# Input rows laid out turned by the host, a second weight chunk in quarters, and memory row factors kept for the third block

## The chip, the core and the metric

The kernel runs on one core of a Trainium2 chip. The metric is the device time of one execution in microseconds (us). The engines that matter here are TensorE (PE in the profile; PEld is its weight load), VectorE (DVE), ScalarE (ACT), GpSimd (POOL), and SyncE (SP), which issues all loads. Loads are moved by 16 DMA engines. Tiles live in SBUF, results of PE in eight PSUM banks.

## The reference

The program is a small two-layer model over one sequence of 256 rows with 1024 features, and 256 rows of memory that every layer attends to:

```python
def rms_norm(x, gain):
    xf = x.astype(jnp.float32)
    y = xf * lax.rsqrt(jnp.mean(xf * xf, axis=-1, keepdims=True) + RMS_EPS)
    return (y * gain.astype(jnp.float32)).astype(x.dtype)

def memory_cross_attention(h, m, w_q, w_kv, w_o, q_norm, k_norm):
    k, v = _split(m @ w_kv, (MEM_HEADS * MEM_HEAD_DIM, MEM_HEADS * MEM_HEAD_DIM))
    ...

def first_block(x, mem, ...):
    for i in range(DEPTH):                      # DEPTH = 2
        h = rms_norm(x, norm_mix[i])
        if i % 2 == 0:
            x = x + dsa_moba_mixer(h, ...)       # block 1: its first product is h @ ab_w_in, 1024 x 2472
        else:
            x = x + nsa_mixer(h, ...)            # block 3
        x = x + memory_cross_attention(rms_norm(x, norm_mem[i]), rms_norm(mem, norm_mem_src[i]), ...)
        x = x + swiglu(rms_norm(x, norm_ffn[i]), ffn_w_in[i], ffn_w_out[i])    # with memory: blocks 2 and 4
    return x

def reference(x, mem, positions, ...):
    x = first_block(x, mem, positions, ...)
    return second_block(x, ...)                  # blocks 5 to 8: two layers of branches and a feed-forward
```

x and mem enter a product only after rms_norm, and the mean square of a memory row is the same in both layers, since mem never changes. The kernel makes the memory's keys and values of layer 0 in block 1, those of layer 1 in block 3.

## The kernel before

**Products.** Every product is computed in three matmuls of split numbers: a weight w is rounded to w_hi by ACT (L143) and the remainder w_lo = w - w_hi is formed by DVE (L144); the features are split in the same way into h_hi and h_lo. PE then adds h_hi w_hi, h_hi w_lo and h_lo w_hi (L456 to L458 in `Project`, L890 to L892 in `MemoryRows`). Here a group is a feature tile of 128 features and a tile of 128 rows; the 256 rows are two tiles.

**Weights.** `Weights` cuts the weight matrices into chunks of 1 MB (four feature tiles by 512 columns). SP loads the chunks in program order into four raw slots; ACT (`round_to`) and DVE (`cut_to`) fill three slots of halves ahead of PE. A chunk is 24 matmuls of 512 columns. Chunk c goes to ACT when it has landed and the chunk that used its slot is consumed. `FirstChunk` (L208 to L249) handles chunk 0 apart: two loads of half a chunk, and four quarters of 512 columns that ACT rounds (L232) and DVE cuts (L240) one by one, so that PE can begin on the first.

**Features.** `Features` makes h_hi and h_lo of 256 rows. PE turns the rows by 16 transposes into PSUM (`turn`, L279), ACT scales by the gain and rounds (L297), DVE takes the remainder (L303). The row factor of rms_norm is not multiplied in there: ACT squares the rows and sums (L290), three small POOL operations (L312 to L318) make the factor, and it is applied when a product is copied out of its bank (L470 on ACT, L484 on DVE).

**Block 1**, `block_dsa_moba`, is where the program starts. SP loads x, the gains, chunk 0 in halves, chunks 1 to 3, a gain, the positions, the memory rows, then the other chunks as slots come free (`load_all`). `Project` takes two chunks for each block of 512 output columns: chunks 0 and 1 give the first block, 2 and 3 the second. PE does 16 dummy transposes (L1400), turns x, and does the chunks; what it does between chunks is written by hand: after chunk 1 the memory rows are turned, after chunk 3 the index heads are turned (L393, `turn_index`), and the index scores (L1410) follow later. On ACT the order is: features and chunk 0's quarters, chunk 1, the squares of x, chunk 2, the sines of the rope tables (L1036, L1037), the first copy out (L470), chunk 3, the memory rows (L297) and their squares, chunk 4. On DVE: features and quarters, chunk 1, the rope tables (L1051 to L1069, a chain of small steps), chunk 2, the copy out (L484), chunk 3, the memory rows (L303), chunk 4. On POOL the factors of x come first, then the memsets of the rope frequencies (L1031), for which DVE's rope tables wait. All queues run in order: what stands behind a waiting instruction waits with it.

**Block 3**, `block_nsa`, has memory rows of its own again: SP loads them (L870), ACT squares them, POOL makes the factors, PE turns them (L279) ahead of small matmuls (L2323), ACT and DVE split them (L297, L303), and `MemoryRows.pe` (L890) uses them. POOL's head norm (L674), DVE's use of it (L656) and small matmuls of compressed tokens (L2268) stand near that work.

## Time and profile before

| | |
|---|---|
| median of 3 runs | 1661.8 us (1661.35 to 1661.95) |
| span of the profiled execution | 1659.6 us |
| PE busy | 1619.1 us, 98% |
| DVE busy | 1096.3 us, 66% |
| ACT busy | 891.3 us, 54% |
| POOL busy | 421.5 us, 25% |
| read from memory | 262.52 MB |

The span is the time in which the profiler saw the core's instructions; the device time of a run holds a little more, 2.2 us at the median. Times in rows count from the start of the span. A row of the timeline gives the start, the busy time, the engine, the line, the operation, its output and inputs, and how many instructions it sums up; what stands in brackets is how long the engine was idle just before, and what ended that.

### The profile page before, as it was taken

Reading aid. Unit: us, or ns where it says so; the run is one execution under the profiler, and the core shown is the slowest. Engines: PE = TensorE matmul, PEld = TensorE weight load, DVE = VectorE, ACT = ScalarE, POOL = GpSimd, SP = SyncE. Lnnn points to the kernel's source line nnn. Section 1 sums busy time; section 2 is a strip of 40 time slices with the busy share of each in tenths; the row PEclk is TensorE's granted clock in tenths of the full one; section 3 lists DMA queues with packets and bytes.
Section 4 is the critical chain, followed back from the end, with each engine's and each line's share of the span. In section 5 each row is a group of like instructions: output and inputs, shape, how many; then the busy total and the mean of one; then the engine's idle time right before and its main releaser. Section 6 shows DMA issues by size and latency. Waiting matters only on the chain. (4 is left out here: it accounts for less than half of the span.)

```text
span 1659.6 us, 26949 instructions
## 1 busy us (share of the span) xinstructions
PE 1619.1 (98%) x10929; PEld 1462.8 (88%) x10929; DVE 1096.3 (66%) x1546; ACT 891.3 (54%) x1401; POOL 421.5 (25%) x460
## 2 busy tenths in 40 slices
PE   8999999999999999999999999999999999999999
PEld 7767899987887889998889998999888999999997
DVE  6875665645576665655577768777646876867763
ACT  6465554434455555443456746566445684756652
POOL 2500100002341120000147802244204690214430
PEclk9999999999999999999999999999999999999999
DMA  7523376556330236665555444766556444376652
GB/s 278 174 77 101 103 205 194 185 197 213 99 135 27 77 102 172 185 186 193 174 195 164 147 133 147 189 185 190 181 154 220 159 153 130 131 204 187 190 179 76
DMA packets 287067, 265.30 MB, mean 160 GB/s; under 512 B 12256, under 2 KB 247520, under 8 KB 286944
## 3 DMA queue, kind: packets, MB, share of 16 engines
q1 hardware_dynamic: 286944, 263.59, 50.8%
q8 instruction: 86, 1.41, 0.4%
q14 instruction: 37, 0.30, 0.1%
HBM read 262.52 MB, written 1.05 MB: 159 GB/s over the span
## 5 line engine op out<-in xcount | busy, mean ns | idle before, releaser
L144 DVE TENSOR_TENSOR w_lo<-w_raw,w_hi 128x2048 fp32r<-128x2048 f32 (+2 forms) x244 | 565.8, 2321 | 288.6 <-ACT w_hi L143 283.6
L143 ACT ACTIVATE w_hi<-w_raw 128x2048 fp32r<-128x2048 f32 (+2 forms) x244 | 462.9, 1902 | 214.6 <-PE bank L529 125.5
L1873 PE MATMUL bank<-h_hi,w_hi 128*128 128x256 f32 x1984 | 565.5, 285 | 4.7 <-issue 1.2
L1874 PE MATMUL bank<-h_lo,w_hi 128*128 128x256 f32 x1984 | 561.3, 283 | 0.0
L1875 PE MATMUL bank<-h_hi,w_lo 128*128 128x256 f32 x1984 | 561.2, 283 | 0.0
L1873 PEld LDWEIGHTS bank<-h_hi,w_hi 128*128 128x128 f32 x1984 | 380.5, 192 | 8.2 <-issue 7.5
L1874 PEld LDWEIGHTS bank<-h_lo,w_hi 128*128 128x128 f32 x1984 | 380.7, 192 | 0.1
L1875 PEld LDWEIGHTS bank<-h_hi,w_lo 128*128 128x128 f32 x1984 | 380.6, 192 | 0.0
L456 PE MATMUL bank<-w_hi,h_hi 128*128 128x512 f32 (+1 forms) x288 | 113.4, 394 | 5.4 <-DVE w_lo L144 3.3
L2953 POOL TENSOR_TENSOR cffn_hidden<-cffn_conv 128x256 f32<-128x256 f32 x44 | 73.7, 1675 | 155.5 <-ACT cffn_conv L2984 155.5
L457 PE MATMUL bank<-w_lo,h_hi 128*128 128x512 f32 (+1 forms) x288 | 111.9, 388 | 0.0
L458 PE MATMUL bank<-w_hi,h_lo 128*128 128x512 f32 (+1 forms) x288 | 111.7, 388 | 0.0
L2531 POOL TENSOR_TENSOR mix_conv<-mix_conv,mix_gates 128x512 f32<-128x512 f32 x60 | 105.2, 1752 | 24.4 <-ACT mix_gates L2568 17.2
L1770 ACT ACTIVATE mf_gate<-mf_gate 128x256 f32<-128x256 f32 x44 | 18.4, 418 | 129.8 <-DVE mf_gate L1819 129.8
L3018 DVE SCALAR_TENSOR_TENSOR cffn_conv<-cffn_before,cffn_cols,cffn_conv 128x255 f32<-128x255 f32 x176 | 75.0, 488 | 0.0
L456 PEld LDWEIGHTS bank<-w_hi,h_hi 128*128 128x128 f32 x288 | 54.2, 188 | 18.8 <-DVE w_lo L144 4.2
L458 PEld LDWEIGHTS bank<-w_hi,h_lo 128*128 128x128 f32 x288 | 54.2, 188 | 10.9
L457 PEld LDWEIGHTS bank<-w_lo,h_hi 128*128 128x128 f32 x288 | 54.2, 188 | 10.1
L3006 DVE TENSOR_TENSOR cffn_before<-bank,cffn_row_factors 128x512 f32<-128x512 f32 x44 | 30.4, 691 | 49.4 <-PE bank L1875 48.7
L2482 POOL MEMSET mix_padded<- 128x572 f32 x2 | 1.2, 577 | 240.4 <-POOLq L1728 187.2
L778 ACT ACTIVATE mix_att<-mix_att,mix_att_stat 128x256 f32<-128x256 f32 x48 | 24.0, 502 | 61.5 <-PE bank L750 40.0
L526 PE MATMUL bank<-w_lo,cffn_wide_hi 128*128 128x512 f32 x144 | 56.0, 389 | 0.0
(447 smaller groups left out, 2858.0 us busy)
## 6 DMA issues: line engine op xcount, KB each, us to landing
w_raw<-in_w_in SPq DMA_DIRECT2D x48, 1024.0 KB, 5.0
w_raw<-in_ffn_w_in SPq DMA_DIRECT2D x88, 512.0 KB, 5.0
w_raw<-in_w_up SPq DMA_DIRECT2D x88, 512.0 KB, 5.2
w_raw<-in_ffn_w_out SPq DMA_DIRECT2D x22, 1024.0 KB, 4.9
w_raw<-in_w_down SPq DMA_DIRECT2D x22, 1024.0 KB, 5.0
w_raw<-in_nsa_w_in SPq DMA_DIRECT2D x10, 1024.0 KB, 5.2
w_raw<-in_mem_w_kv SPq DMA_DIRECT2D x8, 1024.0 KB, 5.1
w_raw<-in_w_branch SPq DMA_DIRECT2D x8, 1024.0 KB, 5.1
```

Source lines behind the costliest of these rows:

```text
L143: return act.activation(hi, raw, ACT.Copy)
L144: return dve.tensor_tensor(self.lo[:, cut_slot, 0:k * n], raw, hi.bitcast(F32), ALU.subtract)
L456: pe.matmul(bank, x_hi, whi[:, k, :], start=(f == 0), stop=False)
L457: pe.matmul(bank, x_hi, wlo[:, k, :], start=False, stop=False)
L458: ins = pe.matmul(bank, x_lo, whi[:, k, :], start=False, stop=(f == KD - 1))
L526: pe.matmul(self.bank[2 * t + half][:, :], x_hi, wlo[:, k, columns], start=False, stop=False)
L1873: pe.matmul(out, h, hi[:, f, :], start=(f == 0), stop=False)
L1874: pe.matmul(out, h, lo[:, f, :], start=False, stop=False)
L1875: ins = pe.matmul(out, l, hi[:, f, :], start=False, stop=(f == KD - 1))
L2531: pool.tensor_tensor(conv[:, :, :], conv[:, :, :], taps[tap % 4], ALU.add).then_inc(cv_sum, 1)
L2953: pool.tensor_tensor(hidden[:, j % 2, :], conv[:, j % 2, 0, :], conv[:, j % 2, 1, :], ALU.mult)\
L3018: dve.scalar_tensor_tensor(out=dst, in0=src, scalar=tap(2 * side, tile), in1=dst, op0=ALU.mult, op1=ALU.add).then_inc(sides, 1)
```

## The change

The host also passes x and mem laid out turned, as 128 features by 8 tiles by 256 rows (`x_turned`, `mem_turned`). `Features` with `laid` reads such a tile in SBUF instead of the banks, and PE turns neither x nor the memory rows, in block 1 or in block 3. The rows themselves are still loaded in block 1, for the squares and for the residual sum; x's rows now come after chunk 2 in SP's queue, behind both halves of x_turned, chunk 0 and chunk 1. The dummy transposes become 20. `FirstChunk` is made for chunks 0 and 1, so chunk 1 too is loaded in halves and split in quarters; FIRST_ORDER says which features are rounded and cut ahead of which quarter. Chunk 2 is rounded ahead of the squares of x on ACT, behind which there is now a wait for x's rows, and cut ahead of the rope tables on DVE. The memory rows' factors are kept in `mem_stat` beside the memory's keys and values, so block 3 has no squares, no factor steps and no load of the rows (it loads `mem_turned` instead, as many bytes).

```diff
@@ FirstChunk
-    def __init__(self, k, chunk):
-        s, self.w, (self.rows, self.n, sources) = k.sems, k.weights, chunk
+    def __init__(self, k, chunk, c):
+        s, self.w, self.c, (self.rows, self.n, sources) = k.sems, k.weights, c, chunk
...
@@ Features
     def view(self, f):
+        if self.laid is not None:
+            return self.laid[:, f, :]
         return self.k.bank[(self.bank + f // 2) % 8][:, (f % 2) * S:(f % 2) * S + S]
...
         for f in features:
-            if not self.first:
+            if self.laid is not None:
+                if self.landed:
+                    act.wait_ge(self.landed[f // 4], 16)
+            elif not self.first:
                 act.wait_ge(self.turned, self.turns[f // 4])
...
@@ MemoryRows
-    def turn(self, pe):
-        pe.wait_ge(self.rows_in, 16)
-        self.features.turn_all(pe)
-
     def load(self, sp):
-        sp.dma_start(self.rows, self.source.rearrange("(t p) d -> p t d", p=P)).then_inc(self.rows_in, 16)
+        sp.dma_start(self.turned, self.a["mem_turned"]).then_inc(self.turned_in, 16)
+        if self.layer == 0:
+            sp.dma_start(self.rows, self.a["mem"].rearrange("(t p) d -> p t d", p=P)).then_inc(self.rows_in, 16)
...
-                self.features.wait_feature(pe, 1 if f == 0 and self.sums[0] == self.bank else f)
+                self.features.wait_feature(pe, f)
...
@@ block_dsa_moba
+        FIRST_ORDER = [(0, 1, 2), (3,), (4, 5), (6,), (7,), (), (), ()]
...
             def _(sp):
-                sp.dma_start(k.x[:, :, :], a["x"].rearrange("(t p) d -> p t d", p=P)).then_inc(x_in, 16)
                 sp.dma_start(k.gains_1[:, :], a["cols_1"]).then_inc(cols_in, 16)
                 for part in range(2):
-                    first.load(sp, part)
-                for c in range(1, w.EARLY):
-                    w.load(sp, w.chunks[c], w.raw_slot(c), w.early_in[c])
+                    features = slice(4 * part, 4 * part + 4)
+                    sp.dma_start(x_turned[:, features, :], a["x_turned"][:, features, :]).then_inc(x_landed[part], 16)
+                    first[0].load(sp, part)
+                for part in range(2):
+                    first[1].load(sp, part)
+                w.load(sp, w.chunks[2], w.raw_slot(2), w.early_in[2])
+                sp.dma_start(k.x[:, :, :], a["x"].rearrange("(t p) d -> p t d", p=P)).then_inc(x_in, 16)
+                w.load(sp, w.chunks[3], w.raw_slot(3), w.early_in[3])
...
@@ ACT
-                for i in range(3):
-                    rows.round(act, range(2 * i, 2 * i + 2))
-                    first.round(act, i)
-                first.round(act, 3)
-                rows.round(act, range(6, KD))
-                w.round_to(act, 1)
+                for i, features in enumerate(FIRST_ORDER):
+                    rows.round(act, features)
+                    first[i // 4].round(act, i % 4)
+                w.round_to(act, 2)
+                act.wait_ge(x_in, 16)
                 for t in range(T):
                     for part in range(2):
                         rows.square(act, t, part)
-                w.round_to(act, 2)
                 rope_tables.act(act)
...
@@ DVE
+                for i, features in enumerate(FIRST_ORDER):
+                    rows.cut(dve, features)
+                    first[i // 4].split(dve, i % 4)
+                w.cut_to(dve, 2)
                 rope_tables.dve(dve)
...
@@ PE
-                for i in range(16):
+                for i in range(20):
                     pe.transpose(k.bank[i // 4][:, i % 4 * P:i % 4 * P + P], k.ident[:, :], k.ident[:, :])
-                pe.wait_ge(x_in, 16)
-                rows.turn_all(pe)
...
                 def index(pe, j, part):
-                    if (j, part) == (0, 1):
-                        mem.turn(pe)
                     if (j, part) == (1, 1):
-                        pe.wait_ge(mem.features.lo_done, KD)
                         turn_index.pe(pe, lambda pe, i: hn.wait_done(pe, 2) if i < 2 else pe.wait_ge(doubled, 1))
...
@@ block_nsa
-        mem = MemoryRows(k, a, 1, feat[:, 0:8, :].rearrange("p (t a) b -> p t (a b)", t=T),
-                         [double[:, t, :, :].rearrange("p a b -> p (a b)") for t in range(T)], h_hi, h_lo, bank=0,
-                         sums=(0, 1, 3, 3))
+        mem = MemoryRows(k, a, 1, feat[:, 0:8, :], None, None, h_hi, h_lo, sums=(0, 1, 3, 3))
...
-                mem.features.factors(pool, 2)
...
-                        mem.act_square(act)
...
-                mem.turn(pe)
```

What stands in a row on the queues at the start of block 1, by the kernel's lines, shows the moves. SP, before (in_x is x, in_ab_w_in the weights of chunks 0 and on, ab_feat the tile that takes the memory rows):

```order
L1204 DMA x_rows<-in_x 128x2x1024
L1205 DMA gains<-in_cols 128x68
L221 DMA w_raw<-in_ab_w_in 128x2x512 x2
L126 DMA w_raw<-in_ab_w_in 128x4x512 x3
L1210 DMA ab_gain<-in_rows 128x256
L1026 DMA ab_pos_i<-in_positions 128x2
L870 DMA ab_feat<-in_mem 128x2x1024
```

SP, now:

```order
L1213 DMA gains<-in_cols 128x68
L1216 DMA ab_feat<-in_x_turned 128x1024
L221 DMA w_raw<-in_ab_w_in 128x2x512
L1216 DMA ab_feat<-in_x_turned 128x1024
L221 DMA w_raw<-in_ab_w_in 128x2x512 x3
L126 DMA w_raw<-in_ab_w_in 128x4x512
L1221 DMA x_rows<-in_x 128x2x1024
L126 DMA w_raw<-in_ab_w_in 128x4x512
L1223 DMA ab_gain<-in_rows 128x256
L1033 DMA ab_pos_i<-in_positions 128x2
L874 DMA ab_mem_turned<-in_mem_turned 128x2048
L876 DMA ab_feat<-in_mem 128x2x1024
```

x's rows moved from the front to a place between chunks 2 and 3, and two loads of 1 MB are new. ACT from the end of chunk 0's quarters to the round of chunk 4, before (ab_att takes the squares that nobody reads, ab_mem_hi the rounded memory features):

```order
L143 ACTIVATE w_hi<-w_raw 128x2048
L290 ACTIVATE ab_att,row_stat<-x_rows 128x512 x4
L143 ACTIVATE w_hi<-w_raw 128x2048
L1036 ACT_TABLE_LOAD
L1036 ACTIVATE rope_tables<-ab_cos_in 128x32
L1037 ACTIVATE rope_tables<-ab_sin_in 128x32
L470 ACTIVATE ab_proj<-bank,row_stat 128x512
L143 ACTIVATE w_hi<-w_raw 128x2048
L641 ACTIVATE ab_squares<-ab_proj 128x128
L297 ACTIVATE ab_mem_hi<-bank,gains 128x256 x8
L290 ACTIVATE ab_att,ab_mem_stat<-ab_feat 128x1024 x2
L143 ACTIVATE w_hi<-w_raw 128x2048
```

The same stretch of ACT now, from chunk 1's quarters on:

```order
L232 ACTIVATE w_hi<-w_raw 128x512 x4
L143 ACTIVATE w_hi<-w_raw 128x2048
L293 ACTIVATE ab_att,row_stat<-x_rows 128x512 x4
L1043 ACT_TABLE_LOAD
L1043 ACTIVATE rope_tables<-ab_cos_in 128x32
L1044 ACTIVATE rope_tables<-ab_sin_in 128x32
L477 ACTIVATE ab_proj<-bank,row_stat 128x512
L143 ACTIVATE w_hi<-w_raw 128x2048
L648 ACTIVATE ab_squares<-ab_proj 128x128
L303 ACTIVATE ab_mem_hi<-ab_mem_turned,gains 128x256 x8
L293 ACTIVATE ab_att,mem_stat<-ab_feat 128x1024 x2
L143 ACTIVATE w_hi<-w_raw 128x2048
```

The round of chunk 2 moved ahead of the squares of x; that of chunk 3 stands where it stood, behind the sines and the first copy out. DVE from chunk 1 to chunk 3, before (the small steps of the rope tables between):

```order
L144 TENSOR_TENSOR w_lo<-w_raw,w_hi 128x2048
L1051 CAST ab_pos<-ab_pos_i 128x2
L1052 CAST ab_pos<-ab_row_i 128x2
L1054 TENSOR_SCALAR ab_ang<-ab_inv,ab_pos 128x8 x4
L1057 TENSOR_SCALAR ab_turns<-ab_ang 128x32
...
L1069 TENSOR_SCALAR ab_cos_in<-ab_cos_in 128x32
L144 TENSOR_TENSOR w_lo<-w_raw,w_hi 128x2048
L484 TENSOR_SCALAR ab_proj<-bank,row_stat 128x512
L144 TENSOR_TENSOR w_lo<-w_raw,w_hi 128x2048
```

DVE now, from chunk 1's quarters:

```order
L240 TENSOR_TENSOR w_lo<-w_raw,w_hi 128x512 x4
L144 TENSOR_TENSOR w_lo<-w_raw,w_hi 128x2048
L1058 CAST ab_pos<-ab_pos_i 128x2
L1059 CAST ab_pos<-ab_row_i 128x2
L1061 TENSOR_SCALAR ab_ang<-ab_inv,ab_pos 128x8 x4
L1064 TENSOR_SCALAR ab_turns<-ab_ang 128x32
...
L1076 TENSOR_SCALAR ab_cos_in<-ab_cos_in 128x32
L491 TENSOR_SCALAR ab_proj<-bank,row_stat 128x512
L144 TENSOR_TENSOR w_lo<-w_raw,w_hi 128x2048
```

Chunk 2's cut moved from behind the rope tables to ahead of them; chunk 3's stays behind.

## Rows read from the trace of the kernel before

**Rows 1.** The page's head: span, and busy time, share, instructions by engine.

```profile
span 1659.6 us, 26949 instructions
PE 1619.1 (98%) x10929; PEld 1462.8 (88%) x10929; DVE 1096.3 (66%) x1546; ACT 891.3 (54%) x1401; POOL 421.5 (25%) x460
```

**Rows 2.** Timeline of PE, first 45 us: start, busy, instruction, idle before.

```profile
5.81 2.73 PE L279 MATMUL bank<-ident,x_rows 128*128 128x128 f32 x16
10.27 0.47 PE L456 MATMUL bank<-w_hi,h_hi 128*128 128x512 f32 x1 [1.72 <-DVE w_lo L240]
...
17.07 0.50 PE L456 MATMUL bank<-w_hi,h_hi 128*128 128x512 f32 x1 [1.02 <-DVE w_lo L144]
...
22.68 1.91 PE L279 MATMUL bank<-ident,ab_feat 128*128 128x128 f32 x16
...
31.05 0.39 PE L456 MATMUL bank<-w_hi,h_hi 128*128 128x512 f32 x1
...
37.07 0.48 PE L456 MATMUL bank<-w_hi,h_hi 128*128 128x512 f32 x1
...
43.65 0.72 PE L1410 MATMUL bank<-ab_feat 32*128 32x128 f32 x8 [0.89 <-DVE ab_feat L422]
```

**Rows 3.** Loads of chunks 1 to 3 (issue, landing), then windows: PEclk, share, GB/s.

```profile
L126 SPq DMA_DIRECT2D w_raw<-in_ab_w_in x3: 489/574/1427, 2.8 to 3.9; - x3
...
DMA to landing us min/median/max: 8.5/10.7/12.8
...
10.00:15.00 5.00, 4.74 (x21) 3.74 (x22) 4.56 (x11) 5.00 (x9) 0.00 (x0) 1.00 1.05 387
```

**Rows 4.** Timeline of ACT, first 35 us.

```profile
8.50 0.63 ACT L232 ACTIVATE w_hi<-w_raw 128x512 fp32r<-128x512 f32 x1
...
14.54 0.67 ACT L290 ACTIVATE ab_att<-x_rows 128x512 f32<-128x512 f32 x1
...
23.13 0.23 ACT L1036 ACTIVATE rope_tables<-ab_cos_in 128x32 f32<-128x32 f32 x1 [2.90 <-DVE ab_cos_in L1069]
...
23.95 1.90 ACT L143 ACTIVATE w_hi<-w_raw 128x2048 fp32r<-128x2048 f32 x1
...
31.33 1.97 ACT L143 ACTIVATE w_hi<-w_raw 128x2048 fp32r<-128x2048 f32 x1
```

**Rows 5.** Timeline of POOL and DVE, first 45 us.

```profile
17.20 0.20 POOL L312 TENSOR_TENSOR row_stat<-row_stat 128x2 f32<-128x2 f32 x1 [15.18 <-ACT ab_att L290]
...
18.92 0.49 DVE L1051 CAST ab_pos<-ab_pos_i 128x2 f32<-128x2 int32 x1 [1.91 <-POOL ab_inv L1031]
...
26.00 2.29 DVE L144 TENSOR_TENSOR w_lo<-w_raw,w_hi 128x2048 fp32r<-128x2048 f32 x1
...
43.09 0.42 DVE L422 COPY ab_feat<-bank 128x256 f32<-128x256 f32 x1
```

**Rows 6.** Block 3: windows (PEclk, third from the end), and PE's timeline.

```profile
424.00:427.00 3.00, 3.00 (x21) 2.74 (x20) 1.10 (x1) 0.00 (x0) 1.85 (x2) 0.50 0.24 49
...
472.00:475.00 3.00, 3.00 (x8) 2.34 (x7) 2.96 (x8) 0.85 (x1) 2.71 (x9) 0.50 0.00 0
...
422.10 4.29 PE L2268 MATMUL bank<-nsa_att,nsa_cmp_w 128*64 128x75 f32 x32 [1.42 <-issue]
...
472.07 0.63 PE L891 MATMUL bank<-w_lo,h_hi 128*128 128x512 f32 x1
...
472.50 0.63 PE L892 MATMUL bank<-w_hi,h_lo 128*128 128x512 f32 x1
```

**Rows 7.** Timeline of block 3 near the memory rows, PE and DVE.

```profile
419.49 2.51 DVE L2194 COPY nsa_att<-bank 64x510 f32<-64x510 f32 x4
...
465.59 1.97 PE L279 MATMUL bank<-ident,nsa_feat 128*128 128x128 f32 x16
...
468.84 0.94 DVE L656 TENSOR_TENSOR nsa_proj<-nsa_proj,nsa_hn_stat 128x512 f32<-128x512 f32 x1 [1.53 <-POOL nsa_hn_stat L674]
...
471.57 0.70 PE L890 MATMUL bank<-w_hi,h_hi 128*128 128x512 f32 x1 [0.52 <-DVE h_lo L303]
```

More of the change, by code:

```diff
@@ L251, with __init__ @@
 class Features:
-    def __init__(self, k, name, src, gain, hi, lo, scratch, bank, first=0, stat=None, parts=2):
+    def __init__(self, k, name, src, gain, hi, lo, scratch, bank=0, first=0, stat=None, parts=2, laid=None, landed=()):
         s = k.sems
+        self.laid, self.landed = laid, landed
         self.k, self.src, self.gain, self.hi, self.lo, self.scratch = k, src, gain, hi, lo, scratch
@@ L301, in cut @@
         for f in features:
-            dve.wait_ge(self.hi_done, f - f % 2 + 2 - self.first)
+            dve.wait_ge(self.hi_done, f + 1 if self.laid is not None else f - f % 2 + 2 - self.first)
             dve.scalar_tensor_tensor(out=self.lo[:, f, :], in0=self.view(f), scalar=self.gain[:, f:f + 1],
@@ L442, in pe @@
             for c in range(self.first[j], self.last[j] + 1):
-                if c or self.tiles is None:
+                tiles = self.tiles[c] if self.tiles is not None and c < len(self.tiles) else None
+                if tiles is None:
                     w.wait_cut(pe, c)
@@ L450, in pe @@
                         self.features.wait_feature(pe, f)
-                    if c == 0 and self.tiles is not None:
-                        self.tiles.wait_cut(pe, k)
+                    if tiles is not None:
+                        tiles.wait_cut(pe, k)
                     for t in range(T):
@@ L843, with __init__ @@
 class MemoryRows:
-    def __init__(self, k, a, layer, rows, scratch, hi, lo, bank=4, sums=(3,)):
+    def __init__(self, k, a, layer, turned, rows, scratch, hi, lo, sums=(3,)):
         s = k.sems
-        self.k, self.rows, self.hi, self.lo, self.source = k, rows, hi, lo, a["mem"]
-        stat = k.small("mem_stat", [P, 5, T])
-        self.rows_in, self.summed, self.copied = s("mem_in"), s("mem_summed"), s("mem_copied")
+        self.k, self.layer, self.turned, self.rows, self.hi, self.lo, self.a = k, layer, turned, rows, hi, lo, a
+        self.rows_in, self.turned_in = s("mem_in"), s("mem_turned_in")
+        self.summed, self.copied = s("mem_summed"), s("mem_copied")
         gain = k.gains_1[:, (2 + 4 * layer) * KD:(3 + 4 * layer) * KD]
-        self.features = Features(k, "mem_rows", rows, gain, hi, lo, scratch, bank, stat=stat, parts=1)
-        self.bank, self.sums = bank, sums
+        self.features = Features(k, "mem_rows", rows, gain, hi, lo, scratch, stat=k.mem_stat, parts=1, laid=turned,
+                                 landed=[self.turned_in] * 2)
+        self.sums = sums
     def add_chunks(self, w):
@@ L1121, in block_dsa_moba @@
         gains_in, const = s("gains_in"), s("const")
-        rows = Features(k, "rows", k.x, k.gains_1[:, 0:KD], h_hi, h_lo, k.norm_scratch, 4)
+        x_in, cols_in, filled = s("x_in"), s("cols_in"), s("filled")
+        x_turned, x_landed = feat[:, 8:16, :], [s("x_turned_in0"), s("x_turned_in1")]
+        rows = Features(k, "rows", k.x, k.gains_1[:, 0:KD], h_hi, h_lo, k.norm_scratch, laid=x_turned, landed=x_landed)
         after = Features(k, "after", k.x, k.gains_1[:, KD:2 * KD], h_hi, h_lo, k.norm_scratch, 4)
@@ L1308, in _ @@
             def _(dve):
-                for i in range(3):
-                    rows.cut(dve, range(2 * i, 2 * i + 2))
-                    first.split(dve, i)
-                first.split(dve, 3)
-                rows.cut(dve, range(6, KD))
-                w.cut_to(dve, 1)
+                for i, features in enumerate(FIRST_ORDER):
+                    rows.cut(dve, features)
+                    first[i // 4].split(dve, i % 4)
+                w.cut_to(dve, 2)
                 rope_tables.dve(dve)
```

29 lines of the change are left out of this document (16 added, 13 removed).

## The prediction

> **What bounds the kernel now.** I read the page's head first. The program is one core's chain of matrix work: PE is busy 98% of a span of 1659.6 us [rows 1]. A change can win only what PE waits for or no longer does, and only as far as nothing later takes it back. So I read the places that the diff touches: the first 45 us of block 1, and block 3 around its memory work.
>
> In the first 45 us, PE's timeline gives the stages and its waits [rows 2]. x lands at 5.8, PE turns it until 8.54 and waits 1.72 us for the first features and weights; the products start at 10.27. A chunk is 24 matmuls; chunk 1 runs from 17.07 to 22.68, 5.6 us or 0.23 us a matmul. Chunk 1 waited 1.02 us for DVE's w_lo, then come 1.91 us of memory turns, and chunk 3 starts at 31.05 with no wait beside its row. Chunk 4 starts at 37.07. The index scores at 43.65 wait 0.89 us for DVE's copy at 43.09 [rows 2, 5]; that copy hangs on the end of chunk 3 through the projection's copies.
>
> Loads come next. Issue time plus time to landing of the three whole chunks (2.8 + 8.5, 3.9 + 12.8) gives 11.3 and 16.7 for chunks 1 and 3, so 2.7 us for each MB, in the order of issue; the DMA engines are full (1.05) in 10 to 15 us [rows 3]. A load placed earlier delays by 2.7 us per MB all that is placed behind it.
>
> Last ACT, POOL and DVE, since the rows of x matter there for their mean square. ACT squares x at 14.54, POOL's factors start at 17.20 on the last square, the memsets of the rope frequencies stand behind them, DVE's rope tables start at 18.92 on those memsets, ACT's sines at 23.13 wait for DVE, and ACT rounds chunk 3 at 23.95 only after the sines and a copy [rows 4, 5]. DVE cuts it from 26.00 to 28.29 [rows 5], 2.76 us before PE wants it at 31.05. That slack is what the change spends.
>
> **The change part by part.** The span is 2.2 us shorter than the median of 1661.8 us; I work in the span's times and apply the difference to the median.
>
> *x loaded turned.* PE loses 16 turns, 2.73 us [rows 2], and the wait that followed. In total 1 MB lies ahead of the first half of chunk 0 (half of x_turned, half of the chunk), which is what lay ahead of 5.8 us before. ACT's first rounding of weights, at 8.50 before [rows 4], can then start near 5.9, and from it to the first matmul the old trace takes 10.27 - 8.50 = 1.8 us: first matmul near 7.7, **2.5 us earlier**. The four more dummy transposes cost nothing: at the 2.73 / 16 = 0.17 us of a turn they are 0.7 us, and PE is free from 5.6. With no such cover they would cost those 0.7. ACT and DVE read these features from SBUF now; the nearest rows are the same instructions from PSUM, and a few tenths either way lie under the matmuls of a feature (6 x 0.23 = 1.4 us).
>
> *Chunk 1 in quarters.* Its second half lands at 11.3 as before; the last four quarters need ACT's 0.63 us [rows 4] and something like that on DVE each, so the last is cut near 13.3, and the first well before chunk 0 ends (7.7 + 5.6 = 13.3). The wait of 1.02 goes: chunk 1 starts near 13.4, **3.7 us earlier**, and ends near 19.0.
>
> *Chunk 2 and the turns of the memory rows.* Chunk 2 still lands at 14.0 (11.3 + 2.7); 1.9 us of rounding (the row of chunk 3's) and 2.29 of cutting end at 18.3, under chunk 1. The 1.91 us of turns are gone. Chunk 2 follows chunk 1 at 19.0 and ends near **24.5**.
>
> *Where that gain goes.* x's rows were first in the queue; now gains, x_turned and chunks 0 to 2 are ahead, 4 MB, so they land where chunk 3 landed, at 16.7 [rows 3]. ACT's explicit wait for them stands ahead of the squares, which begin some 0.2 us after the landing (as PE did at 5.81, rows 2), near 16.95 instead of 14.54: 2.4 us later. Behind that wait on ACT are the sines, the copy and chunk 3's rounding; on POOL the factors and the memsets; on DVE, behind its wait for the memsets, the tables and chunk 3's cut. Each keeps its old distance:
> - squares to POOL's factors 17.20 - 14.54 = 2.66: 19.6;
> - POOL to the tables 18.92 - 17.20 = 1.72: 21.3;
> - tables to sines 23.13 - 18.92 = 4.21: 25.5;
> - sines to chunk 3's rounding 0.82, rounding 1.90: 28.3;
> - cut 2.29: **30.6**, and PE can start chunk 3 near 30.7.
>
> Before, it started at 31.05. Of the 6.5 us that PE gained, 0.35 is left; PE stands idle some 6.2 us, from 24.5 to 30.7, for DVE's cut of chunk 3.
>
> *Chunk 4.* It lands later, since turned memory rows and one more MB (x) stand ahead, but its rounding on ACT comes after that of chunk 3, the memory rounds and two squares. From the end of chunk 3's rounding (23.95 + 1.90 = 25.85) to the start of chunk 4's (31.33) are 5.5 us [rows 4]; so at the latest 28.3 + 5.5 = 33.8, rounded 35.7, cut 38.0. Before, PE came to chunk 4 at 37.07, 6.0 us after chunk 3's start, so now it comes at 36.7 and waits up to 1.3 us for chunk 4. That wait is covered by the 0.89 us at the index scores and the 0.35 by which their chain, which goes by the end of chunk 3, comes earlier. Net without the clock: **-0.3**, from 1661.8 to 1661.5.
>
> *The clock.* The 1.72 us of waiting from 8.54 on left the granted clock at 1.00 in 10 to 15 us [rows 2, 3]. But in block 3, 1.42 us of waiting and 32 small matmuls stand ahead of a granted clock of 0.50 in 424 to 427, and 0.52 us of waiting, at 471.57, ahead of 0.50 in 472 to 475 [rows 6, 7]. That is 1.2 GHz. A wait of 6.2 us is much longer than any here, so I take it that chunk 3 starts at half speed. The price is read from the second fall: 8 matmuls in 3.00 us, 0.43 us from one start to the next (472.07, 472.50) instead of 0.23, so 8 x 0.2 = **1.6 us** lost. From below the cost is 0 (the clock isn't lowered, or is back at once), from above all 24 matmuls of chunk 3, 24 x 0.2 = 4.8. I take 1.6, the one row that shows this kind of matmul after a fall. Chunk 3's end goes by it, so the index chain too: -0.3 + 1.6 = **+1.3**.
>
> The Trainium skill, page TensorE: Matmul & The Clock Gate, section HAM oscillation — how this bites in real kernels, says the same against this change: waits on PE between bursts send it back to half speed, and each next burst begins slow. Without that rule and with the first 45 us alone as witness the sum would be 1661.5; with it, 1663.1. No row of this trace has a wait of such length.
>
> *Block 3.* PE loses 16 turns (1.97 us at 465.59), ACT two squares and POOL three small operations. Nothing behind them is waiting for them. The small matmuls that follow on PE may start 1.9 us earlier, but the memory products at 471.57 wait for DVE's h_lo, and DVE stands behind its row at 468.84, which waited 1.53 us for POOL's head norm [rows 7]. That chain doesn't use the memory rows. Earlier, the matmuls at 422.10 wait 1.42 us for DVE's copies (419.49 + 2.51 = 422.00), not for ACT's squares [rows 6, 7]. So 1.9 us more of waiting, and 0 in the sum. Bounds: the whole 1.9 gained, if h_lo isn't what is late; or a longer stretch at half speed, since PE waits 2.4 us there instead of 0.5: at most a second price of 1.6 lost. The loads are as many bytes as before.
>
> **Sum**: -0.3 + 1.6 + 0 = +1.3 us, 1661.8 to **1663.1 us**: PE does 6.6 us less and stands that much longer.
>
> **The rivals.**
> - *No clock cost.* The clock comes back at once, or isn't lowered: 1661.5. For it: no fall after 1.72 us at the start. Against: two falls in block 3 after less.
> - *Slower: the low clock holds for all of chunk 3.* Then 24 matmuls lose 4.8 us, and the index chain comes 4.8 - 0.35 = 4.45 us later: **1666.2**. It is slower by over 3.3 us from (3.3 + 0.35) / 0.2 = 18 matmuls on. For it: chunk 3 is the first work after a full stop. Against: the fall at 472 was over after 8.
> - *Faster: x's rows don't hold chunk 3.* If x lands by some 13 us although it is issued behind 4 MB, its chain ends before 28.3 as it did before, and chunk 3 goes on at 25 or 26; then chunk 4 holds PE. That lands four loads of 1 MB behind 16.7 (chunk 3, the memory rows twice, itself), at 27.5, with the small loads between some 28.6; with 1.9 and 2.29 PE starts it at 33 instead of 37.07: -4.1, **1657.7**. For it: everything but x's rows is early enough. Against: the landings go by order of issue [rows 3], and the program waits for x explicitly.
> - *Block 3 pays.* 1.9 us come off there: 1663.1 - 1.9 = 1661.2. Against: the row at 471.57 names h_lo.
>
> The Trainium skill, page DMA: Bandwidth & Descriptors, section Queues, rings and completion order, says that completion is not first in, first out per issuing engine. By that x could land ahead of chunk 2, and the time would go towards the third rival's. Rows 3 here show the landings in order and 2.7 us apart.
>
> **How the numbers follow.** Forecast 1663.1: 0.52; no clock cost: 0.18; block 3 pays: 0.10; slower by the clock: 0.14; faster by an early x: 0.06. A measurement of this kernel can tell about 0.2%, 3.3 us. The first three are all within that: same 0.80, slower 0.14, faster 0.06. The range leaves out the last two cases and takes in the block 3 case without a clock cost (1659.6, nearly) and a second price in block 3 or a somewhat longer low stretch: **1660.0 to 1665.3**.
>
> **What would show it right or wrong.** In the changed trace: PE's first matmul near 7.7, chunk 1 near 13.4, chunk 2 near 19; ACT's squares near 17, DVE's tables near 21, chunk 3's cut near 28.3 to 30.6; on PE a wait of 6 us ahead of chunk 3 with DVE w_lo as its end, a granted clock of about 0.5 right behind it; index scores near 45; in block 3 a wait of over 2 us ahead of the memory products. It is wrong if x's squares start before 15, if chunk 3 starts before 29 or after 32, or if its matmuls start 0.23 us apart from the first.

## The result: 1668.4 us, slower by 0.4%

The changed kernel takes 1668.39 us at the median of 5 runs (1667.06 to 1668.69), the kernel before 1661.79; the ratio is 1.0039, with a 95% interval of 1.0027 to 1.0051. The forecast was 1663.1 us, with a range up to 1665.3. The profiled execution has a span of 1667.0 us, 7.4 more than before; it is the highest of the five runs, so the stages below add up to 7.4 and not to the 6.6 between the medians.

The page's head of the changed kernel, as [rows 1]:

```profile
span 1667.0 us, 26864 instructions
PE 1620.5 (97%) x10885; PEld 1460.6 (88%) x10885; DVE 1097.8 (66%) x1549; ACT 891.1 (53%) x1400; POOL 420.7 (25%) x457
```

TensorE has 44 instructions less and is busy 1.4 us longer. Its timeline in the first 47 us, as [rows 2]:

```profile
8.06 0.47 PE L463 MATMUL bank<-w_hi,h_hi 128*128 128x512 f32 x1 [1.65 <-DVE w_lo L240]
...
13.90 0.39 PE L463 MATMUL bank<-w_hi,h_hi 128*128 128x512 f32 x1
...
19.34 0.43 PE L463 MATMUL bank<-w_hi,h_hi 128*128 128x512 f32 x1
...
31.33 0.79 PE L463 MATMUL bank<-w_hi,h_hi 128*128 128x512 f32 x1 [6.33 <-DVE w_lo L144]
31.92 0.63 PE L464 MATMUL bank<-w_lo,h_hi 128*128 128x512 f32 x1
32.35 0.63 PE L465 MATMUL bank<-w_hi,h_lo 128*128 128x512 f32 x1
...
46.49 0.72 PE L1417 MATMUL bank<-ab_feat 32*128 32x128 f32 x8 [0.85 <-DVE ab_feat L428]
```

Chunk 2 starts 6.1 us earlier than before (19.34 against 25.48), and chunk 3 0.28 later, behind a wait of 6.33 us. Its matmuls start 0.43 us apart. The granted clock there (third from the end of a row of the windows):

```profile
25.00:30.00 5.00, 0.00 (x0) 0.00 (x0) 2.80 (x7) 3.88 (x8) 2.56 (x7) 0.97 1.05 399
30.00:33.00 3.00, 1.67 (x4) 1.38 (x5) 3.00 (x7) 3.00 (x7) 2.92 (x6) 0.50 1.03 356
33.00:36.00 3.00, 3.00 (x8) 2.32 (x8) 1.78 (x5) 3.00 (x5) 1.73 (x4) 0.50 0.95 358
36.00:40.00 4.00, 4.00 (x21) 3.29 (x21) 2.76 (x2) 0.58 (x2) 0.00 (x0) 0.93 0.17 29
```

So 12 of chunk 3's 24 matmuls ran at the 1.2 GHz level, and the index scores come at 46.49 instead of 43.65, **2.84 us** later. What held chunk 3 is the chain of [rows 4, 5], in the timelines of ACT and DVE:

```profile
17.53 0.63 ACT L293 ACTIVATE ab_att<-x_rows 128x512 f32<-128x512 f32 x1 [0.64 <-DMA x_rows<-in_x]
...
26.12 0.23 ACT L1043 ACTIVATE rope_tables<-ab_cos_in 128x32 f32<-128x32 f32 x1 [4.72 <-DVE ab_cos_in L1076]
...
26.94 1.90 ACT L143 ACTIVATE w_hi<-w_raw 128x2048 fp32r<-128x2048 f32 x1
...
21.90 0.49 DVE L1058 CAST ab_pos<-ab_pos_i 128x2 f32<-128x2 int32 x1 [2.69 <-POOL ab_inv L1038]
...
28.87 2.40 DVE L144 TENSOR_TENSOR w_lo<-w_raw,w_hi 128x2048 fp32r<-128x2048 f32 x1 [2.00 <-ACT w_hi L143]
```

The 2.84 us in block 1 are the first piece of the 7.4. I then lined up TensorE's matmuls of both traces one by one and followed the lead from stage to stage. It grows in three more places: by **1.65 us** in the down product of the first feed-forward (block 2), by about **1.3** in block 3, of which 1.0 between 464 and 482 us, and by **1.65** in the down product of block 4. From there to the end it doesn't change. The two down products (the second product of a feed-forward, `wide_hi` and `wide_lo` with its weights) have the same instructions in both kernels.

DVE's remainders of weights (one for each 24 matmuls) show the pace in a down product, here of before and then of the changed kernel:

```profile
340.17 2.29 DVE L144 TENSOR_TENSOR w_lo<-w_raw,w_hi 128x2048 fp32r<-128x2048 f32 x1 [3.14 <-ACT w_hi L143]
...
372.81 2.29 DVE L144 TENSOR_TENSOR w_lo<-w_raw,w_hi 128x2048 fp32r<-128x2048 f32 x1 [3.15 <-ACT w_hi L143]
```

```profile
343.35 2.29 DVE L144 TENSOR_TENSOR w_lo<-w_raw,w_hi 128x2048 fp32r<-128x2048 f32 x1 [3.31 <-ACT w_hi L143]
...
371.35 2.29 DVE L144 TENSOR_TENSOR w_lo<-w_raw,w_hi 128x2048 fp32r<-128x2048 f32 x1 [3.31 <-ACT w_hi L143]
```

Between the two rows lie six chunks before and five in the changed kernel. Six chunks in 32.64 us are 5.44 each, 0.2267 us a matmul; five in 28.00 are 5.60, 0.2333. The granted clock in that stage is 1.00 in both.

In block 3 the rows of the changed kernel that answer to [rows 7] are:

```profile
475.35 4.32 DVE L309 SCALAR_TENSOR_TENSOR h_lo<-nsa_feat,gains,h_hi 128x256 fp32r<-128x256 f32 x8
...
476.18 0.76 PE L896 MATMUL bank<-w_hi,h_hi 128*128 128x512 f32 x1 [1.00 <-DVE h_lo L309]
...
485.02 1.09 PE L2329 MATMUL bank<-ident,nsa_cmp_probs 128*128 128x128 f32 x8 [1.23 <-DVE nsa_cmp_probs L2227]
```

Before, the eight remainders took 3.21 us and the transposes of the probabilities waited 0.30 us:

```profile
470.57 3.21 DVE L303 SCALAR_TENSOR_TENSOR h_lo<-bank,gains,h_hi 128x256 fp32r<-128x256 f32 x8
...
479.20 1.09 PE L2330 MATMUL bank<-ident,nsa_cmp_probs 128*128 128x128 f32 x8 [0.30 <-DVE nsa_cmp_probs L2227]
```

### The profile page after: what moved, and what is told of

It is laid out like the page before. It is cut to its first block and busy times, and to the rows that moved or that the text cites. A ratio compares the mean times of both kernels' runs of the same rounds, so it can differ in the third digit from the quotient of the medians.

```text
span 1667.0 us, 26864 instructions
## 1 busy us (share of the span) xinstructions
PE 1620.5 (97%) x10885; PEld 1460.6 (88%) x10885; DVE 1097.8 (66%) x1549; ACT 891.1 (53%) x1400; POOL 420.7 (25%) x457
## 5 line engine op out<-in xcount | busy, mean ns | idle before, releaser
L144 DVE TENSOR_TENSOR w_lo<-w_raw,w_hi 128x2048 fp32r<-128x2048 f32 x243 | 563.3, 2320 | 294.8 <-ACT w_hi L143 289.7
L143 ACT ACTIVATE w_hi<-w_raw 128x2048 fp32r<-128x2048 f32 x243 | 461.1, 1902 | 218.5 <-PE bank L536 128.2
L533 PE MATMUL bank<-w_lo,mf_wide_hi 128*128 128x512 f32 x144 | 57.3, 398 | 0.0
```

The lines of the kernel that those rows point to most:

```text
L143: return act.activation(hi, raw, ACT.Copy)
L144: return dve.tensor_tensor(self.lo[:, cut_slot, 0:k * n], raw, hi.bitcast(F32), ALU.subtract)
L533: pe.matmul(self.bank[2 * t + half][:, :], x_hi, wlo[:, k, columns], start=False, stop=False)
```

## The experiments

The lead in the text below is how much later a matmul starts than the same matmul of the kernel before.

**Where tiles lie: e1, e2, e5.** `mem_stat` is now kept with the memory's keys and values. It has 40 bytes, takes 64, and stands ahead of all later tiles of blocks 1 to 4, so the hidden tiles of the feed-forward (`wide_hi`, `wide_lo`) moved by 64 bytes. Start addresses in a partition, modulo 256, as the programs have them:

```
             h_hi, h_lo   w_hi, w_lo   wide_hi, wide_lo
before       128          128          128
changed      128          128          192
e1_pad       128          128            0
e2_shift     128          128          192
e5_pad256    128          128          128
e8_phase     128          192          192
e10_phase128 128            0            0
e11_phase192 128           64           64
e9_chain_64  128          192          192
```

e1, on the changed kernel:

```diff
-        self.mem_stat = stack.enter_context(self.nc.sbuf_tensor("mem_stat", [P, 5, T], F32))
+        self.mem_stat = stack.enter_context(self.nc.sbuf_tensor("mem_stat", [P, 16, T], F32))
```

> The changed kernel with 128 bytes instead of 40 set aside for the kept row factors, nothing else. Theory (place): the kept factors sit between the memory's keys and values and all later tiles of blocks 1 to 4, so they push the hidden tiles of the two feed-forward stages (wide_hi, wide_lo) 64 bytes on; in these stages alone a matmul starts 0.2333 us after the last instead of 0.2267, which loses 1.65 us in each. With 128 bytes the tiles stand a multiple of 128 bytes from where they stood, so both stages run at 0.227 again: 3.3 us less than the changed kernel, near 1665.1 us. Rival (load): the stages are slower because loads or other engines reach them at another time; then 0.233 stays and the time stays near 1668.4.

Measured: 1667.74 us (1666.26 to 1670.56), against 1664.44 for e5 below. The down product kept a slow pace, 27.88 us for five chunks, 0.2323 a matmul:

```profile
344.02 2.29 DVE L144 TENSOR_TENSOR w_lo<-w_raw,w_hi 128x2048 fp32r<-128x2048 f32 x1 [3.29 <-ACT w_hi L143]
...
371.90 2.29 DVE L144 TENSOR_TENSOR w_lo<-w_raw,w_hi 128x2048 fp32r<-128x2048 f32 x1 [3.30 <-ACT w_hi L143]
```

By itself this run spoke for the rival. e2 went the other way, on the kernel before:

```diff
         self.kv = stack.enter_context(self.nc.sbuf_tensor("mem_kv", [P, T, D], F32))
+        stack.enter_context(self.nc.sbuf_tensor("unused", [P, 16], F32))
```

> The kernel before with a tile of 64 bytes that nobody uses, placed behind the memory's keys and values; no instruction differs. Theory (place): the two feed-forward stages go from 0.227 to 0.233 us a matmul, 1.65 us each, so 3.3 us more than before, near 1665.1 us. Rival (load): nothing else has moved, so 1661.8 us.

Measured: 1664.80 us (1664.34 to 1665.63); ratio to before 1.0023 (1.0014 to 1.0032), with no instruction changed. The pace is that of the changed kernel, five chunks in 28.00:

```profile
340.81 2.29 DVE L144 TENSOR_TENSOR w_lo<-w_raw,w_hi 128x2048 fp32r<-128x2048 f32 x1 [3.31 <-ACT w_hi L143]
...
368.81 2.29 DVE L144 TENSOR_TENSOR w_lo<-w_raw,w_hi 128x2048 fp32r<-128x2048 f32 x1 [3.31 <-ACT w_hi L143]
```

So it is the place of the hidden tiles that costs, and 128 bytes was the wrong step. e5 is e1 with `[P, 32, T]`, 256 bytes:

> As e1_pad, with 256 bytes set aside for the kept row factors. e1_pad left 0.232 us a matmul in the feed-forward stages, so 128 bytes was the wrong step. Over all stages seen so far, those at 0.2267 us have the tile of features and the tile of weights at the same address modulo 256 (128 both); those at 0.231 to 0.236 don't (features at 192, 0, 32, 96, 160). Theory (same address modulo 256): with 256 bytes both stages run at 0.2267 again: 3.3 us less than the changed kernel and near 1664.9 us. Rival (any tile behind the kept factors is in the way of another engine's): still 0.231 or more, near 1668 us.

Measured: 1664.44 us (1663.80 to 1665.57), 3.95 less than the changed kernel at the medians; the pace is 5.44 again:

```profile
343.06 2.29 DVE L144 TENSOR_TENSOR w_lo<-w_raw,w_hi 128x2048 fp32r<-128x2048 f32 x1 [3.14 <-ACT w_hi L143]
...
370.26 2.29 DVE L144 TENSOR_TENSOR w_lo<-w_raw,w_hi 128x2048 fp32r<-128x2048 f32 x1 [3.15 <-ACT w_hi L143]
```

The lead no longer grows in either down product. Against e1 the medians give the same 3.3 us (1667.74 - 1664.44). These 3.3 us are settled.

**The clock: e3.** On e1, ahead of chunk 3:

```diff
                 def index(pe, j, part):
+                    if (j, part) == (1, 0):
+                        for _ in range(50):
+                            pe.transpose(k.bank[7][:, 0:P], k.ident[:, :], k.ident[:, :])
```

> As e1_pad, with 50 transposes of the identity into a bank that nobody reads, on TensorE between chunk 2 and chunk 3, where it otherwise waits 6.3 us. They end before chunk 3's remainder is there, so they delay nothing. Theory (clock): the wait is what lowers the granted clock to 0.50 for 6.8 us, and chunk 3 at half speed loses 2.5 us; with the transposes the clock stays at 1.00 and chunk 3 takes 5.5 us instead of 8.0: 2.5 us less than e1_pad, near 1662.6 us. Rival (cause elsewhere): the clock falls by something else or the matmuls of chunk 3 are held by features or banks: no difference to e1_pad, near 1665.1 us.

Measured: 1665.40 us (1664.92 to 1666.39), 2.3 less than e1. TensorE's timeline and windows:

```profile
24.45 5.62 PE L1425 MATMUL bank<-ident 128*128 128x128 f32 x50
30.91 0.50 PE L463 MATMUL bank<-w_hi,h_hi 128*128 128x512 f32 x1 [0.84 <-DVE w_lo L144]
...
38.17 0.47 PE L463 MATMUL bank<-w_hi,h_hi 128*128 128x512 f32 x1 [0.86 <-DVE w_lo L144]
...
25.00:30.00 5.00, 5.00 (x47) 4.83 (x45) 2.86 (x5) 4.31 (x9) 2.99 (x7) 1.00 1.05 391
30.00:35.00 5.00, 4.16 (x19) 3.40 (x19) 4.37 (x10) 5.00 (x10) 4.24 (x9) 1.00 1.05 384
```

With work in the wait the clock stays at 1.00, and the index scores come 0.13 us later than before, instead of 2.84 in the changed kernel and 3.59 in e1's profile. Chunk 4 is now waited for, 0.86 us, and as the prediction had it that wait is covered.

**Block 3: e4 and e6.** e4 puts transposes of the identity where the memory rows were turned, on e1:

```diff
                 pe.wait_ge(project.copied_d, len(blocks))
+                for i in range(16):
+                    pe.transpose(k.bank[i // 4 % 4][:, i % 4 * P:i % 4 * P + P], k.ident[:, :], k.ident[:, :])
                 pe.wait_ge(ck_feat, 2)
```

> As e1_pad, with 16 transposes of the identity in block 3, in the place where the transposes of the memory rows stood. Theory (clock): taking the turns away gained nothing there, as the memory products wait for the remainders of the features in both, and it doubled the stretch at half clock from 3.4 to 6.8 us, which loses 1.2 us; with TensorE busy there as before the second fall is 3.4 us long again: 1.2 us less than e1_pad, near 1663.9 us. Rival (block 3 is later by other work of the change, such as features read from SBUF): no difference to e1_pad.

Measured: 1668.16 us (1666.70 to 1669.50), no difference to e1 that these runs show. The granted clock's second fall in block 3 was 3.4 us long in the profile, as expected, and the lead still grew by 1.0 us from 464 to 482. So the longer stretch at the low clock is not what costs in block 3. The row that didn't change is DVE's:

```profile
474.98 4.32 DVE L309 SCALAR_TENSOR_TENSOR h_lo<-nsa_feat,gains,h_hi 128x256 fp32r<-128x256 f32 x8
...
484.64 1.09 PE L2331 MATMUL bank<-ident,nsa_cmp_probs 128*128 128x128 f32 x8 [1.51 <-DVE nsa_cmp_probs L2227]
```

e6 undoes the turned load in block 3 alone, on e5 (the kept factors stay; the lines of the helper `MemoryRows` that allow it are left out here):

```diff
-        mem = MemoryRows(k, a, 1, feat[:, 0:8, :], None, None, h_hi, h_lo, sums=(0, 1, 3, 3))
+        mem = MemoryRows(k, a, 1, None, feat[:, 0:8, :].rearrange("p (t a) b -> p t (a b)", t=T), None, h_hi, h_lo,
+                         sums=(0, 1, 3, 3), bank=0)
...
                 pe.wait_ge(project.copied_d, len(blocks))
+                mem.turn(pe)
```

> As e5_pad256, and in block 3 the memory rows are loaded as rows and turned by TensorE again (kept factors stay, so no squares). Theory (remainders from SBUF): in block 3 DVE's eight remainders of the memory features take 4.32 us from SBUF, beside busy POOL, against 3.21 from the banks, and DVE's softmax steps behind them release the transposes that waited 1.23 instead of 0.30 us; with the turns back the eight take 3.2 us, the transposes wait 0.3 us, and the kernel is 1.0 us faster than e5_pad256, near 1663.9 us. Rival (clock): the loss there is the longer stretch at half clock; then e4_warm_third should have shown it, and here the transposes still wait over 1 us and nothing is gained.

```profile
468.11 1.97 PE L282 MATMUL bank<-ident,nsa_feat 128*128 128x128 f32 x16
...
473.08 3.21 DVE L309 SCALAR_TENSOR_TENSOR h_lo<-bank,gains,h_hi 128x256 fp32r<-128x256 f32 x8
...
481.70 1.09 PE L2337 MATMUL bank<-ident,nsa_cmp_probs 128*128 128x128 f32 x8 [0.42 <-DVE nsa_cmp_probs L2234]
```

Measured: 1664.17 us (1663.73 to 1664.54). The remainders are back at 3.21 us, the wait at 0.42, and the lead no longer grows in block 3 (2.52 before it, 2.50 behind it; in e5 2.42 and 3.42). The medians, 1664.17 against e5's 1664.44, show only 0.3 us of the 0.9 between 2.50 and 3.42; the profiles show the stage, the times alone don't settle its size.

**The chain from x's rows: e7.** On e6: positions right behind the gains in SP's queue, POOL's memsets ahead of x's factors, the rope tables on DVE in two parts ahead of chunk 2's cut, chunk 3's rounding ahead of the sines, the memory rows behind chunk 5 and their split behind the second copies (the lines for the last two, and those of e6, are left out).

```diff
                 sp.dma_start(k.gains_1[:, :], a["cols_1"]).then_inc(cols_in, 16)
+                rope_tables.load(sp)
...
-                rope_tables.load(sp)
-                mem.load(sp)
-                w.load_all(sp)
+                w.load_all(sp, 5, mem.load)
...
+                rope_tables.pool(pool)
                 pool.memset(causal[:, :, :], 0.0).then_inc(const, 1)
                 rows.factors(pool, 4)
-                rope_tables.pool(pool)
...
                         rows.square(act, t, part)
+                w.round_to(act, 3)
                 rope_tables.act(act)
...
+                tables = rope_tables.dve(dve)
+                for _ in range(9):
+                    next(tables)
                 for i, features in enumerate(FIRST_ORDER):
                     rows.cut(dve, features)
                     first[i // 4].split(dve, i % 4)
+                for _ in tables:
+                    pass
                 w.cut_to(dve, 2)
-                rope_tables.dve(dve)
```

> As e6_turn_back, and the chain from x's rows to chunk 3 is cut: positions are loaded right after the gains, POOL's memsets stand ahead of x's factors, DVE makes half the rope tables before the first feature and half before chunk 2's remainder, ACT rounds chunk 3 ahead of the sines, the memory rows are loaded behind chunk 5 and split behind the second block's copies. Theory (x chain): chunk 3 waits for nothing but its landing at 20.1 us, is cut at 24.5 and starts near 25 us instead of 31.3; no wait of 6 us, so no half clock; chunk 4 starts between 32 and 34 us instead of 39, the index scores near 39 to 41 us instead of 46.5. The time is 3 to 5 us less than before, 1656.5 to 1658.5 us. Rival (something else is next): head norm and rope on POOL, then chunk 4 or the later memory rows, hold the index scores at 43 us or more, and the time is that of before, 1661 us.

Measured: 1656.70 us (1654.86 to 1658.30); ratio to before 0.9973 (0.9963 to 0.9983). DVE cuts chunk 3 at 22.98, where the changed kernel did at 28.87, and TensorE doesn't wait from its first product to the index scores:

```profile
8.62 0.47 PE L465 MATMUL bank<-w_hi,h_hi 128*128 128x512 f32 x1 [1.97 <-DVE w_lo L242]
...
39.27 0.72 PE L1427 MATMUL bank<-ab_feat 32*128 32x128 f32 x8 [0.88 <-DVE ab_feat L430]
...
22.98 2.28 DVE L146 TENSOR_TENSOR w_lo<-w_raw,w_hi 128x2048 fp32r<-128x2048 f32 x1
...
10.00:13.00 3.00, 3.00 (x9) 2.32 (x8) 2.44 (x7) 2.69 (x6) 0.00 (x0) 0.50 1.06 401
```

The scores come 4.4 us earlier than before, and that gain stays to the end. So the turned rows of block 1 do pay, once nothing that comes from x's rows stands ahead of chunk 3. e7 moves five things at once, so it doesn't say which of them were needed.

Part of the gain was lost on the way. Here the 1.97 us of waiting ahead of the first product were followed by a granted clock of 0.50 (the row of 10 to 13 us); the 1.72 us at that place before and the 1.65 us in the changed kernel were not. Chunk 3 then started at 26.67, though its cut had ended at 25.26 (22.98 + 2.28) and near 25 was expected. At the full clock up to 1.4 us more might be had; no run tried it.

**Which addresses: e8, e10, e11, e9.** e8 is the kernel before with an unused tile of 64 bytes ahead of the raw weights; e10 has 128 bytes, e11 192.

```diff
+        self.keep("unused", [P, 16])
         self.raw = self.keep("w_raw", [P, Weights.RAW, Weights.SIZE])
```

> The kernel before with 64 bytes that nobody uses ahead of the raw weights, so that weights and all tiles behind them stand 64 bytes further on, but the features of 1024 (h_hi, h_lo), which stand ahead, don't. No instruction differs. Theory (weights and features at the same address modulo 256): the feed-forward stages, where both have moved, stay at 0.2267 us a matmul, and the projections from h_hi and h_lo, where one has moved, go to 0.231 to 0.236. Rival (a fixed address modulo 256 is the fast one): both are slow.

Measured: **1636.18 us**, one run, 25 less than before, which nobody expected. The up products are the first products of the feed-forwards of blocks 2, 4, 6 and 8, with 256 columns of features moving. Three windows of e8, in the first up product, a down product and the last up product (TensorE's instructions in the first bracket):

```profile
250.00:290.00 40.00, 40.00 (x342) 40.00 (x341) 24.79 (x29) 17.87 (x21) 0.00 (x0) 1.00 0.72 196
345.00:375.00 30.00, 30.00 (x134) 24.85 (x133) 12.04 (x6) 10.60 (x6) 0.00 (x0) 1.00 0.55 181
...
1500.00:1540.00 40.00, 40.00 (x356) 40.00 (x355) 32.48 (x45) 25.77 (x36) 17.96 (x16) 1.00 0.70 189
```

The same windows before:

```profile
250.00:290.00 40.00, 40.00 (x336) 40.00 (x335) 23.63 (x29) 17.86 (x21) 0.00 (x0) 1.00 0.68 188
345.00:375.00 30.00, 30.00 (x134) 24.86 (x133) 13.65 (x6) 10.16 (x6) 0.00 (x0) 1.00 0.59 201
...
1500.00:1540.00 40.00, 40.00 (x336) 40.00 (x335) 30.96 (x42) 24.29 (x36) 16.94 (x14) 1.00 0.65 182
```

The down product, where both operands moved, keeps its pace (134 in 30 us). The up products, where the weights moved and the features didn't, are faster: 342 and 356 matmuls of 256 columns in 40 us instead of 336. The projections, from h_hi, go from 227 to 229 ns between two starts at the median, slower as expected, though less than the 231 to 236 forecast. So for the products of 512 columns what counts is the two addresses against each other, as the theory said; that there are pairs better than equal ones it didn't say.

> The kernel before with 128 unused bytes ahead of the raw weights: h_hi and h_lo at 128 modulo 256, weights and hidden tiles at 0. Theory (only the distance of the two operands modulo 256 matters): the feed-forward down products, both moved, stay at 0.2267 us; projections from h_hi at 0.229 to 0.236; the up products of 256 columns somewhere between 113 and 120 ns, not above. Rival (the weights' own address matters): the down products slow down too.

Measured: 1659.52 us, one run.

> The kernel before with 192 unused bytes ahead of the raw weights: h_hi and h_lo at 128 modulo 256, weights and hidden tiles at 64. Theory (distance): down products at 0.2267 us, projections slower by 3 to 9 ns, up products at 113 to 120 ns. Rival (the weights' own address): the down products slow down too, and up products are as slow as before, 120 ns.

Measured: 1647.93 us, one run. In both the down product stays at 134 matmuls in 30 us and the projections are slower (232 and 233 to 234 ns at the median). For these products the distance theory holds three times, in e8, e10 and e11.

For the up products the distance is not all. At the median, the starts in the four up products of an execution are 120 ns apart in all four before and in the changed kernel, and 119 in all four of e10. With 64 and with 192 bytes there are two paces, each kept through a whole up product: e8 has 118, 113, 113 and 113 ns, e11 118, 113, 118 and 118. Two windows of e11, in the second and the last up product:

```profile
680.00:720.00 40.00, 40.00 (x355) 40.00 (x354) 25.04 (x32) 19.78 (x24) 0.00 (x0) 1.00 0.69 194
...
1500.00:1540.00 40.00, 40.00 (x342) 40.00 (x341) 31.71 (x44) 25.06 (x37) 16.90 (x14) 1.00 0.68 189
```

So both distances reach both paces, and one run of each does not say which is better: e11's 11.7 us behind e8 come mostly with two more products at the slower pace. What picks the pace, and why the distance matters, no run here shows.

e9 is e7 with e8's 64 bytes.

> e7_chain with 64 unused bytes ahead of the raw weights, as in e8_phase. There the 5952 matmuls of the two feed-forward up products (256 columns, features moving, weights stationary) went from 120 to 115 ns, some 28 us, and the projections lost some 3 us. Theory (the two gains lie in other places): both hold, 1656.7 - 25 = 1632 us, and the starts of block 1 are as in e7_chain. Rival (they share a bound): a faster up product waits for ACT's and DVE's splitting of weights and less than 20 us come off, 1637 us or more.

Measured: 1636.02 us (1631.86 to 1638.21); ratio to before 0.9838 (0.9823 to 0.9853). It beats both kernels, but of the 4.3 us that e7 gained over before little is left beside e8's single run; neither the expected 1632 nor the rival's 1637 or more is the median. Two of five runs lie at 1631.9, where the sum would be. For the profiled run, at 1637.3, the trace shows what is missing. The index scores come 3.8 us earlier than before, so the chain's gain is there. But two of the four up products run at the slower pace, where e8 had one, and such a product takes 4.4 us more (the gain over before in the first up product is 6.7 us here and 2.2 in e8). The first and the last up product of e9:

```profile
250.00:290.00 40.00, 40.00 (x355) 40.00 (x354) 24.53 (x29) 19.62 (x22) 0.00 (x0) 1.00 0.75 208
...
1500.00:1540.00 40.00, 40.00 (x342) 40.00 (x341) 31.72 (x44) 25.06 (x36) 16.90 (x14) 1.00 0.69 189
```

Whether the runs at 1631.9 had one slow product less is not shown, since they have no trace.

## Why the prediction was wrong

Three terms of the sum failed: the place of the tiles, which stood nowhere in it and cost 3.3 us; block 3, put at 0, which cost 1.0; and the clock, put at 1.6, which cost 2.56. The chain of waits in block 1 was right.

**Right.** The chain of block 1, step by step. First matmul 8.06 (forecast 7.7), chunk 1 at 13.90 (13.4), chunk 2 at 19.34 (19.0), squares 17.53 (16.95), tables 21.90 (21.3), chunk 3's rounding 26.94 (26.4), its cut 28.87 (28.3), chunk 3 31.33 (30.7), the wait 6.33 (6.2). The first products are 0.3 to 0.5 us later than forecast. From the squares on all is later by 0.6, since x's rows landed later: issued at 4.7 with 12.8 us to landing they came at 17.5, not at 16.7. So +0.28 stands in place of -0.35. e7 shows by undoing it that this chain ate the gain, and e3 that chunk 4's wait is covered.

**A term mis-sized: the clock.** That the wait lowers the clock was right, and e3 shows it; the term of 1.6 us was taken from a fall that left 8 matmuls slow. Here 12 were slow and it cost 2.56 us (2.84 - 0.28); in e1's profile the same kind of wait cost 3.0, as chunk 3 started 0.62 us later than before and the index scores came 3.59 later. The Trainium skill, page TensorE: Matmul & The Clock Gate, section HAM oscillation — how this bites in real kernels, says that a wait between bursts sends TensorE back to the slow clock, so that the next burst begins slow. This trace agrees: the row of 30 to 33 us stands at 0.50 behind 6.33 us without work. The rival of a slow chunk 3 asked for 18 such matmuls before the kernel would be slower by 0.2%; by itself it was not reached.

**The step that failed in block 3: "0 in the sum".** The prediction asked whether anything waits for the work that went, and found that nothing does. It didn't ask how long the remainders take when their input comes from SBUF; in block 1 it had said "a few tenths either way lie under the matmuls". In block 3 they stand on DVE ahead of the softmax of the compressed scores, which TensorE does wait for. They took 4.32 us instead of 3.21, which moved TensorE by 1.0 us in the profile (e6's profile takes it back; its median shows 0.3 of it).

It takes two things together to slow a remainder. From SBUF with GpSimd idle nothing is lost: in the changed kernel the eight remainders of x's features read SBUF, GpSimd does nothing from 4 to 13 us, and each takes 0.48 us. From a bank with GpSimd busy nothing is lost either: 3.21 us for eight, before and in e6, beside the same GpSimd steps. From SBUF beside these steps each takes 0.54 to 0.68 us. The window, and the remainders of x and of block 3 in the changed kernel (shortest, median and longest in ns):

```profile
4.00:13.00 9.00, 7.32 (x35) 5.98 (x34) 6.55 (x14) 7.12 (x16) 0.00 (x0) 1.00 1.03 386
...
L309 DVE SCALAR_TENSOR_TENSOR h_lo<-ab_feat,gains,h_hi x8: 478/481/484, 5.4 to 11.8; 128x256 fp32r<-128x256 f32 x8
...
L309 DVE SCALAR_TENSOR_TENSOR h_lo<-nsa_feat,gains,h_hi x8: 537/606/681, 475.4 to 479.1; 128x256 fp32r<-128x256 f32 x8
```

The step beside them matters too. The first four of block 3 lie mostly beside GpSimd's steps of 128x128 and take 0.67 to 0.68, the other four beside its steps of 128x64 and take 0.54. The memory rows' remainders in block 1 also lie beside a busy GpSimd, but mostly beside steps of 128x8, and seven of the eight take 0.47 (3.39 us in all).

The Trainium skill, page SBUF — State Buffer, section Who interferes with whom, says that a VectorE instruction with two inputs in SBUF contends with a GpSimd instruction that reads SBUF, and that with at most one such input, outside the two-port modes, it doesn't. From the bank a remainder has one such input, from the turned tile two, and these rows agree. The bound that the prediction gave for block 3 (at most 1.6 lost) held the size, for another reason.

**Not in the sum at all: the place of tiles.** Keeping `mem_stat` was costed as removed work only. What it adds is 64 bytes ahead of every later tile, and the two down products lose 1.65 us each. It is the largest single piece, 3.3 of 7.4 us, and without it the time, e5's 1664.4 us, lies inside the range. No row of the trace of before shows it. The list of allocations shows that the tiles move, but not what that costs.

**The pieces together:** 0.28 + 2.56 in block 1, 1.0 in block 3, 3.3 for the addresses make 7.1 of 7.4; the rest is 0.3 us at the first fall of the clock in block 3, a fall that e1's and e5's profiles don't have.

## What to carry to other kernels

An edit that makes early work faster gives nothing until the inputs that it pushed back in a queue are followed to the last engine they release; here x's rows went behind 4 MB and took sines, copies and a weight chunk with them. Of a step whose input moves from a bank to SBUF, price the instructions that read it, on their own engine, with what runs beside them on other engines and what stands behind them. Compare the addresses of a kernel's tiles before and after an edit as one compares its instructions: a buffer of 40 bytes cost 3.3 us here, more than any other piece. And do not rank two layouts by one run each, where the pace of the same product differs between executions.

## What the runs showed of the chip that was not expected

- The pace of matmuls depends on the start addresses of the moving and the stationary operand against each other, modulo 256 bytes. For 512 columns of moving weights in the down products, equal addresses give 0.2267 us, a stationary tile 64 bytes further 0.2333, 128 bytes further 0.2323 (rows above).
- For 256 columns of moving features, equal addresses give 120 ns and weights 128 bytes further 119. With weights 64 or 192 bytes further an up product runs at 113 or at 118 ns, and keeps that pace through its whole length. With not one instruction changed the whole kernel took 1636.2 us with 64 bytes, 1647.9 with 192 and 1659.5 with 128, one run each, against 1661.3 with equal addresses.
- The 6.33 us wait left 12 matmuls at half clock; 50 transposes of the identity in it kept the clock and made the kernel 2.3 us faster at the medians.
- A VectorE remainder of 128x256 took 0.48 us from SBUF with GpSimd idle, 0.47 from a bank beside a busy GpSimd, and 0.54 to 0.68 from SBUF beside GpSimd steps of 128x64 and 128x128.
